# A decoder layer on one core: projecting queries, keys and values first, with attention heads between the recurrent columns

## What is computed

```
proj = h @ w_in
qkv = proj[..., :c1]            # 12 column blocks of 128
rc = proj[..., c1:c2]           # 14 column blocks
gates = proj[..., c2:]          # 16 column blocks
o_a = attend(q, k, v)
...
xr = (rc + (prev - rc) * rwkv_mu)
wkv_T, y = rwkv_scan(wkv0, rh, decay, kh, vh, kk, a)
...
mixed = sigmoid(gate_a) * (o_a @ w_branch_a) + sigmoid(gate_b) * (o_b @ w_branch_b)
x = x + mixed @ w_out
x = x + moe(rmsnorm(x, ln2), ...)
```

## Time and profile before

| | |
|---|---|
| median of 3 runs | 1387.61 us (1386.1 to 1388.09) |
| profiled execution, own time | 1386.13 us |
| its span, mean granted clock | 1384.1 us, 0.972 |
| PE / DVE / ACT / POOL busy | 1266.3 / 379.6 / 209.2 / 79.5 us |
| HBM read, mean rate | 454.27 MB, 332 GB/s |

### The profile page before, as it was taken

The page is one execution under the profiler, slowest core; times in us unless marked ns, Lnnn a source line. Parts: engine busy times, 40 slices in busy tenths (PEclk is TensorE's granted clock), DMA queues, the critical chain, the costliest instruction groups (busy, mean ns, idle before and its releaser), DMA issues.

```text
span 1384.1 us, 17148 instructions
## 1 busy us (share of the span) xinstructions
PE 1266.3 (91%) x6852; PEld 650.1 (47%) x6852; DVE 379.6 (27%) x707; ACT 209.2 (15%) x421; POOL 79.5 (6%) x48
## 2 busy tenths in 40 slices
PE   5999968898898999999999999999999999899996
PEld 5888845797755433433343333333333333333332
DVE  3042766965453211111111112111121111121112
ACT  2113424112203100100110101010011010011002
POOL 0000161360000000000000000000000000000001
PEclk9999979798899999999999999999999999999999
DMA  7356663013339799999999999999999999999994
GB/s 265 110 180 168 214 207 100 4 43 124 130 131 422 294 427 427 430 426 430 427 429 427 429 429 428 429 427 430 427 429 428 429 429 427 430 427 430 428 429 189
DMA packets 52505, 459.93 MB, mean 332 GB/s; under 512 B 7922, under 2 KB 10300, under 8 KB 27884
## 3 DMA queue, kind: packets, MB, share of 16 engines
q1 hardware_dynamic: 49252, 451.45, 78.7%
q0 software_dynamic: 1888, 5.34, 2.0%
q10 hardware_dynamic: 1328, 2.64, 0.5%
HBM read 454.27 MB, written 5.11 MB: 332 GB/s over the span
## 4 chain that ended last, share of the span: by engine, by line
PE 60%; DMA 26%; DVE 5%; issue 3%; ACT 3%; POOL 1%; SPq 1%; DVEq 0%; ACTq 0%; POOLq 0%
PE ps L1689 20%; DMA work<-in_w_gate_up 12%; DMA ring<-in_w_gate_up 12%; PE ps L1717 11%; PE ps L1293 8%; PE ps L1640 4%; PE ps L1424 3%; PE ps L1672 2%; PE ps L1552 2%; PE ps L1649 2%; PE ps L1493 1%; PE ps L1268 1%; DVE ring L825 1%; PE ps L1543 1%; DVE work L825 1%
## 5 line engine op out<-in xcount | busy, mean ns | idle before, releaser
L1689 PE MATMUL ps<-ring,work 128*64 128x512 f32 x1536 | 341.7, 596 | 21.1 <-DMA ring<-in_w_gate_up 19.7
L1689 PEld LDWEIGHTS ps<-ring,work 128*64 128x64 f32 x1536 | 107.6, 137 | 252.5 <-issue 218.1
L1717 PE MATMUL ps<-ring,work 128*64 128x512 f32 x768 | 170.1, 595 | 18.4 <-ACT work L731 18.4
L1293 PE MATMUL ps<-work,ring 128*128 128x264 f32 x672 | 151.7, 389 | 0.4 <-DVE work L825 0.4
L1202 DVE TENSOR_SCALAR work<-ps 128x512 f32<-128x512 f32 x32 | 22.1, 691 | 464.6 <-PE ps L1689 464.6
L1293 PEld LDWEIGHTS ps<-work,ring 128*128 128x128 f32 x672 | 128.5, 192 | 22.5 <-DVE work L825 0.5
L1689 PE MATMUL ps<-work 128*64 128x512 f32 x512 | 114.4, 596 | 6.2 <-DMA work<-in_w_gate_up 6.2
L1717 PEld LDWEIGHTS ps<-ring,work 128*64 128x64 f32 x768 | 53.4, 137 | 119.7 <-issue 104.0
L1221 DVE SCALAR_TENSOR_TENSOR work<-work 128x512 f32<-128x512 f32 x32 | 24.0, 751 | 309.8 <-ACT work L734 309.8
L726 ACT ACTIVATE work<-work 128x512 f32<-128x512 f32 x32 | 20.1, 629 | 503.6 <-DVE work L1202 503.6
L1640 PEld LDWEIGHTS ps<-work 128*128 128x128 f32 x544 | 66.7, 196 | 29.3 <-DVE work L1206 15.2
(11 more groups left out here) (261 smaller groups left out, 1015.1 us busy)
## 6 DMA issues: line engine op xcount, KB each, us to landing
ring<-in_w_gate_up SPq DMA_DIRECT2D x96, 2048.0 KB, 31.1
ring<-in_w_down SPq DMA_DIRECT2D x48, 2048.0 KB, 35.2
work<-in_w_gate_up SPq DMA_DIRECT2D x32, 2048.0 KB, 30.9
work<-in_w_down SPq DMA_DIRECT2D x16, 2048.0 KB, 34.3
ring<-in_w_in SPq DMA_DIRECT2D x6, 3072.0 KB, 16.0
ring<-in_w_out SPq DMA_DIRECT2D x1, 4096.0 KB, 14.3
ring<-in_w_in SPq DMA_DIRECT2D x2, 1536.0 KB, 9.7
ring<-in_cache_k SPq DMA_DIRECT2D x16, 192.0 KB, 3.2
```

Of the source, the lines that this page charges most:

```text
L1293: last = mm(psum(job, T), WIN[gi % 2][:, k, j * 128:(j + 1) * 128], hT[:, k, :], start=k == 0, stop=k == KD - 1)
L1689: last = mm(PS[bnk][g * 64:g * 64 + 64, :], lhs, UNIT[n % 8][:, w0 + base + g * 512:w0 + base + (g + 1) * 512], start=False, stop=k == KD - 1)
L1717: last = mm(PS[BY][g * 64:g * 64 + 64, :], lhs, UNIT[n % 8][:, w0:w0 + 512], start=k == 0, stop=k == KD - 1)
```

## The change

The job order, and with it every engine's program, is rewritten for the front stage.
- `GROUPS = range(7)`: the blocks are projected in the order `pr0` to `pr41`, so queries, keys and values come first, then the recurrence's blocks, then the gates. Heads, `sst`, `spt`, `pv0`, `pv1` and `sv` stand between `pr13` and `pr26`. The recurrence's input mixing (`shifted`) is done in four pieces on DVE; the six sample vectors `sx` and the four `bo` jobs move behind `pr39` and `pr40`.
- At the start only `ident` and `ln1` are waited for; `par` and `ssT` come after `pr1`. ACT takes half of the `hT` evacuations, and its table is loaded before the input lands.
- Key products are written in place into four buffers `Kb` instead of two (`PROD` is gone); `vn`, `kn`, `qB`, softmax buffers move to other places in SBUF, and `svn` is one piece.
- On SP the loads of cached keys come at once after the fourth bias input, then the broadcast queries `qB` (from ACT's queue to SP's), then the third weight group, and behind it the new key rows. The later weight groups stand between the loads of cached keys and values.
- On POOL `kv_zero` is set by two memsets; `B3` is read back before the store of the shift rows.
- On DVE the sums of the sample recurrence (`sample_sum`) stand earlier: `u` 0 behind the first masks, `y` 0 before `A2`.

```diff
-GROUPS = [2, 3, 4, 0, 1, 5, 6]
+GROUPS = range(7)
...
-        qB = view(RING, 6144, NB, 512)
-        Kb = [view(RING, 18432 + 1536 * i, 3, 512) for i in range(2)]
-        PROD = [view(RING, 10240, 3, 512), view(RING, 23040, 3, 512)]
+        qB = [view(WORK, at, 2, 512) for at in (13880, 14904, 15928, 24840)]
+        Kb = [view(RING, 18432 + 1536 * i, 3, 512) for i in range(4)]
...
             sp.wait_ge(S_("kv_zero"), 1)
-            for b in range(2):
+            for b in range(4):
                 load_cached(Kb[b], A["cache_k"], b, f"ld_k{b}")
+            sp.wait_ge(S_("st_qn"), 16)
+            for i in range(NB // 2):
+                load(qB[i], qn_d[2 * i:2 * i + 2].unsqueeze(0).broadcast_to([128, 2, 512]), f"ld_qB{i}")
+            load(own, A["c_own"], "ld_own")
+            wait_pe("pr5")
+            load_win(2)
             after(sp, "kn2")
-            for b in range(2):
+            for b in range(4):
                 load_new(Kb[b], kn, b, f"ld_k{b}")
...
-            for b in range(2, NB):
-                sp.wait_ge(S_("pool_prod"), b - 1)
+            for b in range(4, NB):
+                sp.wait_ge(S_("s_red"), b - 3)
...
+                if b == 5:
+                    wait_pe("pr11")
+                    load_win(3)
...
+            wait_pe("pr17")
+            load_win(4)
+            wait_pe("pv0")
+            for v in range(4, NB):
                 load_v(v)
+            wait_pe("pr23")
+            load_win(5)
+            wait_pe("pr29")
+            load_win(6)
...
+            pool.wait_ge(full[bank["hT21"]], turn["hT21"])
+            G_(nc.gpsimd.memset(RING[96:128, 20480:21504], 0.0))
+            G_.ready(nc.gpsimd.memset(RING[96:128, 23552:24576], 0.0), "kv_zero", 1)
...
-                G_.ready(nc.gpsimd.tensor_tensor(PROD[b % 2], Kb[b % 2],
-                                                 bc(qB[:, b, :], 1, 3), ALU.mult), "pool_prod", b + 1)
+                G_.ready(nc.gpsimd.tensor_tensor(Kb[b % 4], Kb[b % 4],
+                                                 bc(qB[b // 2][:, b % 2, :], 1, 3), ALU.mult), "pool_prod", b + 1)
...
+            dve.wait_ge(S_("st_qn"), 16)
+            for b in range(4):
+                reduce_b(b)
+            dve.wait_ge(S_("ld_B3"), 32)
+            score(0)
+            reduce_b(4)
+            score(1)
+            normalise(0)
...
-            pe.wait_ge(S_("ld_par"), 16 * 9)
+            pe.wait_ge(S_("ld_ident"), 32)
+            transposes("ln1T", [par[P_LN1:P_LN1 + 8, :]], 8)
...
+            project(9, 12)
+            natural("vn", 8)
+            project(13, 13)
+            score(0)
+            score(1)
+            project(14, 14)
+            turn_probs(0)
+            score(2)
+            project(15, 16)
+            turn_probs(1)
+            score(3)
```

More of the change, by code:

```diff
@@ new lines, in _ @@
+            project(19, 19)
+            turned(3)
+            act.wait_ge(S_("s_scores"), 1)
+            A_.ready(nc.scalar.activation(s64[:64], s64[:64], ACT.Exp, bias=nms[:64], accum_out=lss[:64]), "s_probs", 1)
+            exponents(5)
+            project(20, 20)
+            act.wait_ge(S_("pts_zero"), 1)
+            take(act, "spt")
+            for t in range(3):
+                ins = nc.scalar.activation(pts[:KT[t], t, :, 0:H], psum("spt", 3, NB, H)[:KT[t], t], ACT.Copy)
+                A_.free(ins, "spt") if t == 2 else A_(ins)
@@ new lines, in _ @@
+            score(4)
+            take(dve, "sst")
+            V.free(v.scalar_tensor_tensor(s64[:64], psum("sst", NKEY, parts=64), SCALE, biasS[:64], ALU.mult, ALU.add), "sst")
+            V.ready(v.tensor_reduce(nms[:64], s64[:64], AX.X, ALU.max, negate=True), "s_scores", 1)
+            normalise(3)
+            score(5)
+            after(dve, "ssT")
+            V(shifted(0, 4))
+            dve.wait_ge(S_("s_probs"), 1)
+            V(v.reciprocal(ris[:64], lss[:64]))
+            V.ready(v.tensor_scalar(s64[:64], s64[:64], ris[:64], None, ALU.mult), "s_pn", 1)
@@ L1296, in _ @@
-            project(2, 3, 4)
-            pe.wait_ge(S_("ld_mats"), 16)
-            pe.wait_ge(S_("relb64"), 1)
-            give("bvp")
-            done(mm(psum("bvp", NREL, parts=H), relb[:32, :], hot_p[:32], start=True, stop=True), "bvp")
-            give("bvs")
-            done(mm(psum("bvs", NKEY, parts=64), relb64[:32].rearrange("p a b -> p (a b)"), hot_s[:32], start=True, stop=True), "bvs")
-            for g in range(4):
-                transposes(f"sh{g}", [rcT[:, c, S - 1:T] for c in range(4 * g, min(4 * g + 4, CR))], 128, NB + 1)
@@ new lines, in _ @@
+            project(0, 1)
+            pe.wait_ge(S_("ld_par"), 16 * 8)
+            transposes("par", [par[:P_N, :]], P_N)
+            pe.wait_ge(S_("ld_ss"), 16)
+            transposes("ssT", [ss[:NB, c * 128:(c + 1) * 128] for c in range(CR)], NB)
+            project(2, 3)
+            pe.wait_ge(S_("ld_mats"), 16)
+            pe.wait_ge(S_("relb64"), 1)
+            give("bvp")
+            done(mm(psum("bvp", NREL, parts=H), relb[:32, :], hot_p[:32], start=True, stop=True), "bvp")
+            give("bvs")
@@ new lines, in _ @@
+            done(mm(psum("bvs", NKEY, parts=64), relb64[:32].rearrange("p a b -> p (a b)"), hot_s[:32], start=True, stop=True), "bvs")
+            project(4, 4)
+            after(pe, *[f"pr{c}" for c in range(4)])
+            transposes("qn", [qkvT[:, c, S:T] for c in range(4)], 128, NB)
+            project(5, 8)
+            natural("kn", 4)
+            project(9, 12)
+            natural("vn", 8)
+            project(13, 13)
+            score(0)
+            score(1)
+            project(14, 14)
@@ new lines, in _ @@
+            turn_probs(0)
+            score(2)
+            project(15, 16)
+            turn_probs(1)
+            score(3)
+            project(17, 17)
+            attend(0)
+            pe.wait_ge(S_("s_red"), NB)
+            give("sst")
+            for t in range(3):
+                last = nc.tensor.transpose(PS[bank["sst"]][:64, KO[t]:KO[t] + KT[t]], scs[:KT[t], t, :], C["ident"][:KT[t], :KT[t]])
+            done(last, "sst")
+            project(18, 18)
+            turn_probs(2)
+            score(4)
@@ new lines, in _ @@
+            project(19, 19)
+            turn_probs(3)
+            score(5)
+            project(20, 20)
+            attend(1)
+            pe.wait_ge(S_("s_pn"), 1)
+            give("spt")
+            for t in range(3):
+                last = nc.tensor.transpose(PS[bank["spt"]][:KT[t], t * 64:t * 64 + 64], s64[:64, KO[t]:KO[t] + KT[t]], C["ident"][:64, :64])
+            done(last, "spt")
+            project(21, 21)
+            turn_probs(4)
+            score(6)
+            decode(0)
```

505 lines of the change are left out of this document (247 added, 258 removed).

## The result

The changed kernel takes 1400.58 us (median of four runs, 1396.9 to 1401.49) against 1387.24 before (four runs, 1386.1 to 1388.09): 1.0098 times the time, 95% interval 1.0082 to 1.0115. It is slower, as forecast (1396, range 1378 to 1404). The profiled execution took 1401.22 us with a span of 1399.4, 15.3 more than the span before.

What follows compares the result with a forecast made beforehand. The experts' weight stream sets the end and shifts with the front stage, PE work with one hole; tV 11.9 us later less 3 after it gives 1395.0 us profiled, 1396 on the median, range 1378 to 1404.

Steps and rivals of the forecast that it cites:

- Head: Kernel start: PE waits only for `ident` and `ln1`, so the first projection comes at 15.2 us instead of 20.75.
- The bias write: POOL's write of the bias table, issued at 35.5 us, lands 35.8 us later and decides when the heads can start.
- What the same engines do meanwhile: During the bias write, SP's loads stand still on eight of 16 DMA engines; 2.75 MB wait, first key product (P0) 91.5.
- rival 3: Worse than the sum: full queues keep SP from issuing, or heads wait singly for DVE; 1404 to 1408 us, chance 0.10.
- P0 to `pt0`: From POOL's first key product to the first head's transposes: 21.4 us, against 29 before.
- Behind `pt0`: From the first head's transposes to tV: 130.7 us of PE work, a 1.5 wait and 1.8 for slow restart.
- The restart: PE's slow clock after its waits near the first head costs about 1.8 us, half of the earlier hole's 3.9.
- `s_pn` by nothing: Among the heads, DVE stays ahead of PE throughout, at `s_pn` with no margin.
- After tV: Stretch behind tV: earlier sample sums and a warm PE gain 3 us, bounds 0 and 6.
- the four operations: Four DVE operations behind `A2`, 2.26 us each beside POOL's work, run free at 0.7 each, 6 us less on DVE.
- Sum: Whole kernel: 11.9 us later at tV, 3 gained after, so 1386.13 + 8.9 = 1395.0 us for the profiled execution.
- Rival 1: The bias write holds nothing up: first key product (P0) at 73.3, tV 228.7, 1377 us; chance 0.17.

Runs made afterwards that it cites:

- e5: Changed kernel with the eight `ln1` rows loaded behind the first weight piece, as in the kernel before: 1408.86 us, 1.0168 of before.
- e1: Changed kernel with the bias table written in 32 copies (0.39 MB) instead of 128 and read back in eight loads: 1385.87 us, 0.9997 of before.
- e3: Changed kernel with the bias table written in 256 copies (3.1 MB) instead of 128: 1430.42 us, 1.0317 of before.
- e10: Changed kernel with the same 1.57 MB bias table computed on and written from 32 partitions instead of 8, read back in eight loads: 1384.28 us, 0.9984 of before.
- e8: Changed kernel with SP issuing the third weight group ahead of the twelve cached-key loads: 1406.77 us, 1.0153 of before.
- e7: Changed kernel with sample sums `u` 0 and `y` 0 placed on DVE where the kernel before has them: 1398.83 us, 1.0100 of before.
- e2: Kernel before the change, with the 32-copy bias table and its eight loads back: 1387.0 us, 1.0000 of before.
- e9: e1 plus third weight group in two halves, the first ahead of the query broadcasts, and new key rows issued by ACT: 1376.83 us, 0.9921 of before.
- e6: Changed kernel with the same 1.57 MB bias write issued from ACT's queue instead of POOL's: 1406.03 us, 1.0130 of before.

## Why the prediction was right, point by point

- *Head*: 15.2 predicted, 14.76 measured; e5 shows that the early `ln1` rows are its cause.
- *The bias write*: issue at 35.5 predicted, 35.38 measured; landing after 35.8 predicted, 36.4 measured. That it decides when the heads start is shown by e1, e3 and e10.
- *What the same engines do meanwhile*: this step gave the right time by a wrong picture. It said that what SP issues gets through on eight engines and stands still on the other eight, so that at the write's end half of the group, queries and more, 2.75 MB, would wait. In fact the group was issued only at 70.97, 1.1 us before POOL was released by the write's end, so all of its 3 MB were still to come, beside the read-back's 1.57, the rest of the queries and the stores of the new keys: 6.93 MB moved in 71:92, 5.36 of them q1's. Two errors cancel: about twice as much of q1 was left as I counted, and it all moved at 330 GB/s, where I had given q1's two parts 116 and 213. The group landed at 91.09 (90.4 predicted) and P0 came at 91.42 (91.5); that they agree so closely is luck. "Stands still" was too strong as well: in 46:70 q1 passed 644 packets beside q0's 244, and e8 shows the shared engines creeping. What I had put into rival 3, SP kept from issuing, is what the chain shows, at a price of its own of nearly nothing against the forecast.
- *P0 to `pt0`*: 21.4 predicted, 21.7 measured here and 21.6 to 21.7 in e1, e3, e5 to e10 where P0 decided.
- *Behind `pt0`*: 134.0 predicted (130.7 + 1.5 + 1.8), 138.5 measured. This term was mis-sized. The restart cost 3.9 and not 1.8: from `pt0` to the end of two projections it took 12.34 us (113.09 to 125.43) where the same jobs warm take 8.4, at a granted clock of 0.50 in 113:120. That is all of what the slow clock had cost in the hole before, of which I had taken half. And "`s_pn` by nothing" failed: PE waited 1.80 us for it at 147.80 (1.79 to 1.80 in each of the experiments on the changed kernel). The projection behind took 5.52 instead of 3.8, at a granted clock of 0.72 in 147.8:154; in e7, with the same code and the same wait, it took 3.83, and over the ten profiles of changed code 5.3 to 5.5 in four and 3.83 in the rest, so these 1.7 us belong to the execution. Together 5.6; the work itself came out some 1 us shorter than 130.7.

```profile
148.42 3.83 PE L1341 MATMUL ps<-work,ring 128*128 128x264 f32 x16
```

- *After tV*: -3 predicted, -1.5 measured, and neither can be told: the stretch scatters by 5.7 us between profiles of the changed code (164.5 to 170.12), and the code before took 171.64 and, in e2, 167.55. That the four operations would run free was wrong: they took 7.06 us, 1.77 each, since POOL's second half had come to stand beside them.

```profile
283.92 7.06 DVE L864 TENSOR_TENSOR ring<-work,ring 128x512 f32<-128x512 f32 x4
```
```profile
285.32 2.35 POOL L830 TENSOR_TENSOR work<-work 128x1024 f32<-128x1024 f32 x1 [4.34 <-DMA work<-in_state_wkv]
```

- *Sum*: 1395.0 predicted for one execution, 1401.22 measured: 0.2 at `pt0`, 4.5 behind it, 1.5 after tV. The first expert load came at 421.72 where I had said 415.
- *Rival 1* (the write holds nothing up: P0 at 73.3, 1377) is wrong of this kernel, but e10 realises it: P0 at 74.98, a median of 1384.28. Its profiled execution took 1376.38 us, which meets the rival's 1377 by luck: tV came at 232.61 and not 228.7, and it is the fastest of ten. So even with the write cured the change as it stands is worth nothing that can be told on the median; e9, with the small write and the other order of issue, brings 0.8%.

What stays open: how much of SP's stand is a full queue and how much something else at issue; why each engine moved the write from 8 partitions at 7 GB/s and from 32 at 17.5; and whether the partitions or the outermost dimension in DRAM did it.

## What to carry to other kernels

Before moving work ahead of a transfer, ask how that transfer is laid out: a write of 1.57 MB out of 8 partitions took 36 us, alone or beside others, and 12 out of 32, and whatever was issued behind or beside it came late, while nothing had hung on it before. Small rows that an engine waits for don't belong behind a 3 MB load in the same queue: another queue for 8 KB, halves of the load and its first half issued earlier brought 9 us together. And when the first of two branches is freed, look which is second: PE's first wait shrank by 11.6 us in e8, and the kernel became slower.

## What the runs showed of the hardware that was not expected

The same code takes different times behind tV, and the granted clock differs with them. From the first expert load to the load that begins the steady cycle it is 132.3 us in e1 (400.17 to 532.42) and 127.3 in e10 (397.14 to 524.46). The windows of these stretches, e1's and then e10's:

```profile
400.20:440.20 40.00, 36.71 (x133) 19.16 (x132) 10.41 (x28) 10.29 (x20) 0.00 (x0) 0.91 0.98 393
440.20:450.20 10.00, 10.00 (x36) 6.18 (x36) 6.57 (x31) 1.57 (x7) 0.00 (x0) 0.50 0.38 161
```
```profile
397.10:437.10 40.00, 36.71 (x147) 19.96 (x145) 11.16 (x33) 10.68 (x22) 0.00 (x0) 0.96 1.00 403
437.10:447.10 10.00, 8.84 (x57) 5.27 (x58) 6.84 (x30) 3.62 (x13) 0.00 (x0) 1.00 0.32 134
```

In e1 TensorE ran at its lower level (0.50, 1.2 GHz) for ten microseconds between the router and the first experts, behind short waits for DVE, and in e10 at the full one. Such falls come and go between executions: e1's ten runs lie between 1378.05 and 1389.85 us and e10's between 1376.38 and 1392.5, the fastest of these with a mean granted clock of 0.976 and the slowest with 0.963.

The stretch between `pt0` and tV has such a place too, behind a wait of 1.50 us that every version has. The changed kernel and then e5:

```profile
190.75 4.99 PE L1463 MATMUL ps<-work 64*128 64x264 f32 x24 [1.50 <-issue]
```
```profile
195.67 8.07 PE L1463 MATMUL ps<-work 64*128 64x264 f32 x24 [1.50 <-issue]
```

The same 24 matmuls took 4.99 us in seven of the ten profiles of changed code, and 8.07, 8.08 and 7.99 in e5, e3 and e6, with a granted clock of 0.62 to 0.66 over the nine or ten microseconds around them. A term of 3 us behind `pt0` can't be read from one profile of this kernel.
